# A hybrid delta-rule and pooling block: lowest doubling level on 32x32 diagonal tiles, and first projection tiles run between token turns

## The chip, the core and the metric
One core of a Trainium2 chip runs the kernel. The metric is device time in microseconds (us) of one execution. Engines: TensorE (PE), VectorE (DVE), ScalarE (ACT), GpSimd (POOL), SyncE (SP, which issues most DMAs).

## What is computed
A block on 1024 tokens of width 1024, with 16 meta tokens ahead of them, all float32: a mixer (gated delta rule plus a pooling branch), a gated MLP of width 2816, and a last norm. Of the mixer, per chunk of 64 rows (the kernel takes two such chunks, 128 rows, at a time), the part that the change touches:
```python
lower = jnp.where(strict, jnp.einsum('bhncd,bhnsd->bhncs', kb, k) * decay, 0.0)
tinv = lax.linalg.triangular_solve(lower + eye, eye, left_side=True, lower=True, unit_diagonal=True)
u = jnp.einsum('bhncs,bhnsv->bhncv', tinv, v * beta[..., None])
w = jnp.einsum('bhncs,bhnsd->bhncd', tinv, kb * jnp.exp(g)[..., None])
```
and in front of it `u = rms_norm(h)`, `proj = u @ w_in` (8 tiles of 128 columns each of q, k, v, after a causal convolution of 4 taps and SiLU; beta and decay rates; z; pool input; two gates), and behind it `y = g_a * y_a + g_b * y_b` and `y @ w_out`.

## The kernel before, in words
**Precision and units.** Each float32 factor is split into a high and a low part; a product is three matmuls: high by high, high by low, low by high. `unit` (line 702, matmul line 709) makes one weight tile of 128 features times one block of 342 to 348 tokens: 8 x 3 = 24 matmuls. A tile has three blocks. ScalarE makes the high part of a weight tile (`w_high`, line 1029), GpSimd the low (`w_low`, line 605).

**Front.** Nine groups of tokens (the meta tokens and eight of 128) are normed: ScalarE sums squares and takes the root (lines 1033, 1035), VectorE scales into xs (lines 1372, 1374), TensorE transposes (line 722), ScalarE copies to u_hi (line 1054), VectorE makes u_lo (line 1386). Then TensorE runs tile AB (beta and decay), and 24 q, k, v tiles (`project`, line 738) with a turn of the tile before behind each (`turn`, line 744), then four pool tiles. The preparation of chunk 0 (`FIRST_PLAN`) follows, interleaved with the pool products.

**Loop.** Eight iterations. Each runs the recurrence of chunk i (steps P1, V, O, SU, OT) and the preparation of chunk i+1, in the order of STEPS: P1, TKN, V, TKB, GROW, KK, TQ, TKG, O, SU, QK, TQD, OT, X0, Y0, X1, Y1, X2, Y2. Between the steps TensorE runs pieces (8, 9 or 6 of the 72 matmuls of three k ranges) of nine z and gate projection units, as many behind a step as FILLS (line 133) says. Units 3 to 5 are the first gate: ScalarE takes their sigmoid (line 1234), and behind unit 5 VectorE multiplies zs by gs (line 1618).

**The inverse.** KK gives at_m, the strictly lower product, 128x128 per head for 8 heads. Its eight 16x16 diagonal blocks per head are inverted by forward substitution on GpSimd (`substitute`, line 638; 64 rows, one per head and block). They go there and back through DRAM: SyncE's `invert` (line 466) stores 8 blocks, loads them as rows, stores the solutions and loads 8 blocks into bd, whose other elements are zero. Chunk 0 takes one block alone, since all rows but the last 16 are padding. From 16 to 128 there are three doubling levels, each a product X and a product Y: level 0 joins blocks of 16 into 32 (X0, Y0), level 1 gives 64, level 2 gives 128. X0 = at_m by bd, Y0 = X0 (masked to level 0, nmx) by rr, each a full 128x128 product per head (`product`, MATMUL line 814, 8 MATMULs in two halves of 4, each as two passes: 16 in the trace). rr is bd transposed in 32x32 squares by VectorE (line 1511). X1 and Y1 use 32-column tiles on 32 MATMULs and 48 in the trace (lines 840, 848, 850); X2 and Y2 use 64-column ones (lines 853, 856). Steps are ordered between engines by semaphores: s_bd (block load landed), s_rr (rr transposed), s_ps (product in PSUM), s_ev (its result read and stored), s_tt, s_rd, s_gfree.

```python
elif name == "X0":
    pe.wait_ge(s_bd, 16 + 16 * BLKS * c)
    each([done["KK"]], product(at_m, bd))
elif name == "Y0":
    pe.wait_ge(s_rr, c)
    each([done["X0"]], product(nmx, rr))
```

## Time and profile before
| what | value |
|---|---|
| median of 3 runs (range) | 1842.59 us (1842.28 to 1844.46) |
| the profiled execution | 1844.31 us |
| its span in the profile | 1842.5 us |
| TensorE busy | 1753.2 us, 95% |
| VectorE, ScalarE, GpSimd busy | 951.0, 634.5, 485.8 us |
| mean granted clock of TensorE | 0.987 |
| one loop iteration | 61.3 us, of which TensorE is busy 59.88 |

All durations below come from the one profiled execution; what of its time lies outside the span is 1.8 us. The busy share of an engine is an average; what a stage waits for is read from the chain of waits and the timelines.

### The profile page before, as it was taken

To read this page: it belongs to the slowest core of one execution; us is meant where nothing else is said; L and a number is where in the kernel's file an instruction comes from. 1 tells how busy PE (TensorE), PEld (TensorE's weight loads), DVE (VectorE), ACT (ScalarE), POOL (GpSimd) and SP (SyncE) were. 2 spreads that over 40 slices of the span, in tenths; PEclk is the share of its full clock that TensorE was granted. 3 is DMA by queue.
4 is the path that set the end of the run, shared out by engine and by line. 5 is a ranking of instruction groups with operands and counts; after the bars stand their busy time and mean duration, and the time that the engine had idled before them with its cause. 6 is when DMAs were issued, how large, how long until landed. Compare 5 with 4: busy or idle time off the path is not lost.

```text
span 1842.5 us, 30292 instructions
## 1 busy us (share of the span) xinstructions
PE 1753.2 (95%) x11793; PEld 1680.6 (91%) x11793; DVE 951.0 (52%) x1068; ACT 634.5 (34%) x1026; POOL 485.8 (26%) x468
## 2 busy tenths in 40 slices
PE   5999999986999999999978989999999999999997
PEld 4999999985999999999978989899899999999996
DVE  5344545562556655665553256454564554455457
ACT  6544443344353335333522243112222122122213
POOL 3222222123333434343411113212212122122120
PEclk9999999998999999999989999999999999999999
DMA  6133323224223422342377111111111111111112
GB/s 185 56 90 88 94 84 97 86 81 149 64 74 105 117 63 74 105 117 63 74 239 229 35 35 58 46 34 57 46 34 57 46 34 59 44 46 57 34 46 91
DMA packets 189850, 147.00 MB, mean 80 GB/s; under 512 B 22940, under 2 KB 178115, under 8 KB 188660
## 3 DMA queue, kind: packets, MB, share of 16 engines
q1 hardware_dynamic: 148740, 114.88, 21.4%
q10 hardware_dynamic: 40848, 31.49, 5.5%
q8 instruction: 25, 0.41, 0.1%
q0 software_dynamic: 224, 0.12, 0.0%
q14 instruction: 13, 0.11, 0.0%
HBM read 109.72 MB, written 36.74 MB: 79 GB/s over the span
## 4 chain that ended last, share of the span: by engine, by line
PE 85%; DVE 5%; issue 3%; DMA 2%; ACT 2%; POOL 1%; DVEq 1%; POOLq 1%; SPq 0%; ACTq 0%
PE gb L709 60%; PE db L987 12%; PE db L814 5%; PE db L811 2%; PE db L750 1%; DMA yo<-ot_d 1%; PE db L866 1%; PE db L865 1%; DVE hx L1677 1%; DVE nmx L1539 1%; DVE form L1466 0%; PE db L940 0%; DVE fino L1783 0%; PE db L722 0%; ACT hx L1033 0%
## 5 line engine op out<-in xcount | busy, mean ns | idle before, releaser
L709 PE MATMUL gb<-u_hi,w_hi 128*128 128x342 f32 (+2 forms) x2520 | 824.3, 327 | 18.6 <-ACT ht L1275 7.4
L709 PE MATMUL gb<-u_lo,w_hi 128*128 128x342 f32 (+2 forms) x2520 | 810.5, 322 | 0.0
L709 PE MATMUL gb<-u_hi,w_lo 128*128 128x342 f32 (+2 forms) x2520 | 807.4, 320 | 0.0
L605 POOL TENSOR_TENSOR w_lo<-w_raw,w_hi 128x1024 fp32r<-128x1024 f32 x128 | 338.2, 2648 | 1082.3 <-ACT w_hi L1029 1082.3
L709 PEld LDWEIGHTS gb<-u_hi,w_hi 128*128 128x128 f32 x2520 | 478.3, 190 | 22.1 <-issue 19.3
L709 PEld LDWEIGHTS gb<-u_lo,w_hi 128*128 128x128 f32 x2520 | 478.4, 190 | 0.5
L709 PEld LDWEIGHTS gb<-u_hi,w_lo 128*128 128x128 f32 x2520 | 477.8, 190 | 0.0
L1749 DVE TENSOR_TENSOR h<-h,db 128x512 f32<-128x512 f32 x176 | 117.1, 684 | 59.0 <-PE db L987 58.6
L987 PE MATMUL db<-w_hi,a_hi 128*128 128x512 f32 x352 | 140.7, 400 | 2.9 <-DVE a_lo L1773 2.9
L1029 ACT ACTIVATE w_hi<-w_raw 128x1024 fp32r<-128x1024 f32 x128 | 133.6, 1052 | 18.1 <-ACT tm L1098 13.4
L987 PE MATMUL db<-w_hi,a_lo 128*128 128x512 f32 x352 | 139.7, 397 | 0.0
L987 PE MATMUL db<-w_lo,a_hi 128*128 128x512 f32 x352 | 139.6, 397 | 0.0
L1410 DVE SCALAR_TENSOR_TENSOR cacc<-xb,prm,cacc 128x1040 f32<-128x1040 f32 x72 | 109.0, 1514 | 11.3 <-issue 10.6
L1316 ACT ACTIVATE a_hi<-cv 128x1024 fp32r<-128x1024 f32 x21 | 22.3, 1060 | 249.0 <-PE db L987 202.1
L1301 ACT ACTIVATE xv<-gb 128x342 f32<-128x342 f32 x63 | 28.8, 456 | 188.0 <-PE gb L709 188.0
L1703 DVE TENSOR_SCALAR cg<-xg,prm 128x1024 f32<-128x1024 f32 x22 | 16.6, 754 | 140.3 <-ACT xg L1301 135.7
L1407 DVE TENSOR_SCALAR cacc<-xb,prm 128x1040 f32<-128x1040 f32 x24 | 18.3, 762 | 133.9 <-ACT xb L1117 133.9
L1234 ACT ACTIVATE gs<-gb 128x342 f32<-128x342 f32 x48 | 21.9, 456 | 189.7 <-PE gb L709 189.7
L987 PEld LDWEIGHTS db<-w_hi,a_hi 128*128 128x128 f32 x352 | 66.6, 189 | 21.8 <-DVE h L1749 3.6
L1117 ACT ACTIVATE xb<-gb 128x346 f32<-128x346 f32 (+1 forms) x72 | 33.0, 459 | 144.8 <-PE gb L709 144.1
L987 PEld LDWEIGHTS db<-w_hi,a_lo 128*128 128x128 f32 x352 | 66.6, 189 | 15.9
L987 PEld LDWEIGHTS db<-w_lo,a_hi 128*128 128x128 f32 x352 | 66.5, 189 | 15.0
(226 smaller groups left out, 1962.6 us busy)
## 6 DMA issues: line engine op xcount, KB each, us to landing
w_raw<-in_w_in SPq DMA_DIRECT2D x53, 512.0 KB, 3.9
w_raw<-in_w_up SPq DMA_DIRECT2D x44, 512.0 KB, 3.8
qkv_d<-tm ACTq DMA_DIRECT2D x24, 576.0 KB, 3.1
tk<-qkv_d SPq DMA_DIRECT2D x9, 1536.0 KB, 8.5
w_raw<-in_w_down SPq DMA_DIRECT2D x22, 512.0 KB, 3.3
ot_d<-ots ACTq DMA_DIRECT2D x9, 512.0 KB, 3.2
yb_d<-ybs ACTq DMA_DIRECT2D x8, 513.0 KB, 3.8
yl<-yb_d SPq DMA_DIRECT2D x8, 513.0 KB, 5.2
```

The costliest lines, as they stand in the source:

```text
L605: pool.tensor_tensor(w_lo[:, n % SLOTS, :], w_raw[:, n % SLOTS, :], w_hi[:, n % SLOTS, :].bitcast(F32), ALU.subtract).then_inc(s_wlo, 1)
L709: mm = pe.matmul(gb[:, bank, 0:w], wt, u, start=(k == 0 and m == 0), stop=(k == KT - 1 and m == 2))
L811: return lambda o, m: pe.transpose(o, src[:, m, :], ident)
L814: return lambda o, m: pe.matmul(o, a[:, m, :], b[:, m, :], start=True, stop=True)
L987: mm = pe.matmul(db[:, u % 4, :], a, wt, start=(q == 0 and m == 0), stop=(q == 1 and m == 2))
L1029: act.activation(w_hi[:, n % SLOTS, :], w_raw[:, n % SLOTS, :], ACT.Copy).then_inc(s_whi, 1)
L1117: act.activation(xb[:, j % 3, 3 + o:3 + o + w], gb[:, b, 0:w], ACT.Copy).then_inc(s_gfree, 1)
L1234: act.activation(gs[:, o:o + w], gb[:, b, 0:w], ACT.Sigmoid).then_inc(s_gfree, 1)
L1301: act.activation(dst[:, o:o + w], gb[:, b, 0:w], ACT.Copy).then_inc(s_gfree, 1)
L1316: act.activation(a_hi[:, q, :], cv[:, :], ACT.Copy).then_inc(s_ahi, 1)
L1410: t = dve.scalar_tensor_tensor(cacc[:, :], xb[:, slot, j:j + T], tap(j), cacc[:, :], ALU.mult, ALU.add)
L1749: dve.tensor_tensor(dst, dst, db[:, u % 4, :], ALU.add).then_inc(s_dnfree, 1)
```

## The change
**Lowest level.** bd is replaced by a compact bds of [128, 8 heads, 32]: the 32x32 diagonal squares alone. X0 and Y0 become 32x32 products on diagonal tiles of TensorE (4 squares by 8 heads, 32 MATMULs in the code each, 64 counted as two passes); their results lie in one PSUM bank, so VectorE masks or subtracts once for 8 heads on 32 columns. X1 and Y1 use compact squares too, X2 and Y2 64-row and 64-column tiles. Ahead of each half of a tiled step stands a wait on a constant semaphore (`settled`). ScalarE spreads the squares out into rr and tth with six copies (s_rd). X0 waits for s_rr, the transpose of bds on VectorE, where it waited for the load s_bd.
**Transfers.** `invert` stores 4 diagonal squares, loads twice, stores twice, loads once: 9 DMAs for 18. Chunk 0 does all eight blocks where it did one, with the DRAM copy zeroed first; GpSimd clears rr behind the substitution.
**Fills.** Behind OT stand 2 pieces for 5, behind X1 and Y1 2 for 1, behind X2 1 for 0.
**Front.** The first tiles AB, q0 and q1 run block by block from the time that tokens 0 to 3 are normed, with the turns of tokens 4 to 8 between half units. Constants are loaded in two parts, the identity ahead, the rest later. The weight copies on ScalarE (`w_high`) stand behind tokens 2, 3 and 5; sigmoid and softplus for beta and decay move behind q, k, v tiles 15 to 17.

The diff, cut to its core:
```diff
 FILLS = {"P1": 2, "TKN": 0, "V": 1, "TKB": 0, "GROW": 1, "KK": 2, "TQ": 2, "TKG": 2, "O": 2, "SU": 2, "QK": 1,
-         "TQD": 1, "OT": 5, "X0": 1, "Y0": 2, "X1": 1, "Y1": 1, "X2": 0, "Y2": 1}
+         "TQD": 1, "OT": 2, "X0": 1, "Y0": 2, "X1": 2, "Y1": 2, "X2": 1, "Y2": 1}
...
-            sp.dma_start(cst[:, :], consts).then_inc(s_const, 16)
+            sp.dma_start(cst[:, C_ID:C_ID + P], consts[:, C_ID:C_ID + P]).then_inc(s_const, 16)
...
+                if j in (4, 6):
+                    load_w(W_QKV + j // 2 - 2, cols(w_in, (j // 2 - 2) * P))
+            sp.dma_start(cst[:, P:], consts[:, P:]).then_inc(s_const, 16)
...
-            def invert(c, n=BLKS):
...
+            def by_rows(m):
+                return m.rearrange("(h p) c -> p h c", h=HEADS)
+            def sub_blocks(m, e):
+                return m.rearrange("(g e r) (f c) -> e f g r c", e=2, r=SUB, f=2)[e][e]
+            def sub_rows(m, e):
+                n = BLKS * HEADS // 2
+                return m[e * n:(e + 1) * n, :].rearrange("g (r c) -> g r c", r=SUB)
+            def invert(c):
                 sp.wait_ge(s_ev["KK"], 2 * c + 2)
-                for b in range(n):
-                    sp.dma_start(rows(blk_d, b), block(BLKS - n + b, at_m)).then_inc(s_bst, 16)
-                sp.wait_ge(s_bst, stored + 16 * n)
-                sp.dma_start(blk[0:HEADS * n, :], blk_d[0:HEADS * n, :]).then_inc(s_blk, 16)
+                for p in range(P // SQ):
+                    sp.dma_start(by_rows(blk_d)[square(p)], at_m[square(p), :, square(p)]).then_inc(s_bst, 16)
+                sp.wait_ge(s_bst, 16 * (P // SQ) * (c + 1))
+                for e in range(2):
+                    sp.dma_start(sub_rows(blk, e), sub_blocks(blk_d, e)).then_inc(s_blk, 16)
                 sp.wait_ge(s_sol, c + 1)
-                sp.dma_start(sol_d[0:HEADS * n, :], sol[0:HEADS * n, :]).then_inc(s_sst, 16)
-                sp.wait_ge(s_sst, 16 * c + 16)
-                if n < BLKS:
-                    sp.wait_ge(s_zero, 4)
-                for b in range(n):
-                    sp.dma_start(block(BLKS - n + b, bd), rows(sol_d, b)).then_inc(s_bd, 16)
+                for e in range(2):
+                    sp.dma_start(sub_blocks(sol_d, e), sub_rows(sol, e)).then_inc(s_sst, 16)
+                sp.wait_ge(s_sst, 32 * c + 32)
+                sp.dma_start(bds[:, :, :], by_rows(sol_d)).then_inc(s_bd, 16)
...
+            sp.wait_ge(s_zero, 4)
+            sp.dma_start(by_rows(sol_d), bds[:, :, :]).then_inc(s_sz, 16)
+            sp.wait_ge(s_sz, 16)
+            invert(0)
...
-            substitute(0, 1)
+            substitute(0)
             w_low(W_ZG + 2)
             pool.wait_ge(s_gfree, U_ZG)
             pool.wait_ge(s_yb[0], 16 * 4)
             pool.wait_ge(s_yb[1], 16 * 4)
+            pool.memset(rr[:, :, :], 0.0).then_inc(s_zero, 1)
...
+            later = list(range(FIRST_TOKENS[0] + 1, KT + 1))
             for b, (o, w) in enumerate(BLOCKS):
-                unit(W_AB, b, o, w).then_inc(s_g, 1)
+                for n in range(3):
+                    q = 3 * b + n
+                    w_ready(W_AB + n)
+                    if q >= 3:
+                        pe.wait_ge(s_gfree, q - 2)
+                    for hf in range(2):
+                        if later:
+                            turn_tokens(later.pop(0))
+                        if n == 0 and hf == 0:
+                            pe.wait_ge(s_u, 2 * (FIRST_TOKENS[b] + 1))
+                        mm = unit(W_AB + n, n, o, w, 4 * hf, 4 * hf + 4)
+                    mm.then_inc(s_g, 1)
...
+            project(W_QKV + 2, U_QKV + 6, blocks=(0, 1))
+            turn(0, True)
+            project(W_QKV + 2, U_QKV + 6, blocks=(2,))
+            turn(1)
...
+            def settled():
+                pe.wait_ge(s_const, 32)
...
+                def squares(inputs, op):
+                    for h in range(2):
+                        settled()
+                        if freed:
+                            pe.wait_ge(s_ev[freed[0]], freed[1] + h + 1)
+                        for s, v in inputs:
+                            pe.wait_ge(s, v + h + 1)
+                        for m in range(4 * h, 4 * h + 4):
+                            t = op(db[:, bank, m * SQ:(m + 1) * SQ], m)
+                        t.then_inc(s_ps[name], 1)
...
-                    pe.wait_ge(s_bd, 16 + 16 * BLKS * c)
-                    each([done["KK"]], product(at_m, bd))
-                elif name == "Y0":
+                    settled()
                     pe.wait_ge(s_rr, c)
-                    each([done["X0"]], product(nmx, rr))
+                    def lower(o, m):
+                        for p in range(P // SQ):
+                            t = pe.matmul(o[square(p), :], at_m[square(p), m, square(p)], bds[square(p), m, :],
                                           start=True, stop=True)
                         return t
+                    squares([done["KK"]], lower)
+                elif name == "Y0":
+                    def upper(o, m):
+                        for p in range(P // SQ):
+                            t = pe.matmul(o[square(p), :], xms[square(p), m, :], rrs[square(p), m, :],
+                                          start=True, stop=True)
+                        return t
+                    squares([done["X0"]], upper)
...
+                if j in (2, 3, 5):
+                    w_high(W_AB + (2, 3, 5).index(j))
+                elif j == 6:
+                    act.wait_ge(s_hd, 32)
+                    act.wait_ge(s_zero, 3)
+                    ab_taken(0)
...
+                elif name == "Y0":
+                    act.wait_ge(s_ps["V"], 2 * c)
+                    act.wait_ge(s_tt, c)
+                    for p in range(2):
+                        act.activation(tth[square(p), :, square(p)], tts[square(p), :, :], ACT.Copy)
+                    for p in range(P // SQ):
+                        t = act.activation(rr[square(p), :, square(p)], rrs[square(p), :, :], ACT.Copy)
+                    t.then_inc(s_rd, 1)
...
+                elif name == "X0":
+                    dve.wait_ge(s_bd, 16 * c + 16)
+                    dve.wait_ge(s_rd, c)
+                    dve.transpose(rrs[:, :, :], bds[:, :, :]).then_inc(s_rr, 1)
+                    dve.wait_ge(s_ps[name], 2 * c)
+                    dve.tensor_tensor(xms, dsquares(name), cst[:, C_LV:C_LV + SQ].unsqueeze(1).broadcast_to(
+                        [P, HEADS, SQ]), ALU.mult).then_inc(s_ev[name], 2)
+                elif name == "Y0":
+                    dve.wait_ge(s_ps[name], 2 * c)
+                    dve.tensor_tensor(rrs[:, :, :], rrs[:, :, :], dsquares(name), ALU.subtract).then_inc(s_ev[name], 2)
+                    drain()
+                    dve.transpose(tts, rrs[:, :, :]).then_inc(s_tt, 1)
```

VectorE (DVE) in the loop, from the product of QK (qkm) to the first product after X0; before:
```order
L1596 RECIPROCAL tiny<-tiny 128x8 [waits s_ort]
L1599 TENSOR_TENSOR vb<-vb,tiny 128x1024 [waits s_ev_O]
L1617 ISA
L1618 TENSOR_TENSOR zs<-zs,gs 128x1026 [waits s_gfree]
L1550 ISA
L1511 STREAM_TRANSPOSE rr<-bd 128x1024 [waits s_ps_V,s_bd]
L1553 TENSOR_TENSOR nmx<-db,cst 128x512 [waits s_ps_X0] x2
L1558 TENSOR_TENSOR rr<-rr,db 128x512 [waits s_ps_Y0]
```
and now:
```order
L1683 RECIPROCAL tiny<-tiny 128x8 [waits s_ort]
L1686 TENSOR_TENSOR vb<-vb,tiny 128x1024 [waits s_ev_O]
L1708 ISA
L1709 TENSOR_TENSOR zs<-zs,gs 128x1026 [waits s_gfree]
L1628 STREAM_TRANSPOSE rrs<-bds 128x256 [waits s_rd,s_bd]
L1630 TENSOR_TENSOR nmx<-db,cst 128x8x32 [waits s_ps_X0]
L1634 TENSOR_TENSOR rrs<-rrs,db 128x256 [waits s_ps_Y0]
L1636 STREAM_TRANSPOSE nmx<-rrs 128x8x32
```
The transpose stands where it stood, behind the product of zs (zs by gs, which waits for s_gfree, the sigmoid of unit 5). It is 256 columns wide and not 1024, and X0's result is masked in one instruction.

TensorE (PE) around X0 in the loop; db is the product's PSUM bank, gb the projections'. Before:
```order
L709 MATMUL gb<-u_hi,w_hi 128x342
L709 MATMUL gb<-u_lo,w_hi 128x342
L709 MATMUL gb<-u_hi,w_lo 128x342
L831 ISA
L814 MATMUL db<-bd,at_m 128x128 [waits s_ev_KK,s_ev_TQD,s_bd]
L814 MATMUL db<-bd,at_m 128x128 x3
L814 MATMUL db<-bd,at_m 128x128 [waits s_ev_KK,s_ev_TQD]
L814 MATMUL db<-bd,at_m 128x128 x3
L900 REGISTER_ALU
L709 MATMUL gb<-u_hi,w_hi 128x342 [waits s_gfree]
L709 MATMUL gb<-u_lo,w_hi 128x342
```
and now:
```order
L717 MATMUL gb<-u_hi,w_hi 128x342
L717 MATMUL gb<-u_lo,w_hi 128x342
L717 MATMUL gb<-u_hi,w_lo 128x342
L875 MATMUL db<-bds,at_m 32x32 [waits s_ev_TQD,s_const,s_ev_KK,s_rr]
L875 MATMUL db<-bds,at_m 32x32 x15
L875 MATMUL db<-bds,at_m 32x32 [waits s_ev_KK,s_ev_TQD,s_const]
L875 MATMUL db<-bds,at_m 32x32 x15
L708 REGISTER_ALU
L957 REGISTER_ALU [waits s_wlo]
L717 MATMUL gb<-u_hi,w_hi 128x342 [waits s_gfree]
L717 MATMUL gb<-u_lo,w_hi 128x342
L717 MATMUL gb<-u_hi,w_lo 128x342
```
X0 has 32 instructions where it had 8, and waits for s_rr (VectorE's transpose) where it waited for s_bd; ahead of it stand 15 projection matmuls behind OT where there were 39.

TensorE (PE) in the front, from the last token group's transposes (before) and from token group 4's (now) on. Before:
```order
L722 MATMUL db<-cst,xs 128x128 [waits s_u]
L722 MATMUL db<-cst,xs 128x128 x3
L728 MATMUL mb<-cst,prow 128x105 [waits s_prow]
L728 MATMUL mb<-cst,prow 128x88
L728 MATMUL mb<-cst,prow 128x44
L709 MATMUL gb<-u_hi,w_hi 128x346 [waits s_wlo,s_u]
L709 MATMUL gb<-u_lo,w_hi 128x346
L709 MATMUL gb<-u_hi,w_lo 128x346
```
and now:
```order
L729 MATMUL db<-cst,xs 128x128 [waits s_u,s_xs,s_wlo]
L729 MATMUL db<-cst,xs 128x128 x3
L729 MATMUL db<-cst,xs 128x128 [waits s_u]
L729 MATMUL db<-cst,xs 128x128 x3
L717 MATMUL gb<-u_hi,w_hi 128x346 [waits s_u]
L717 MATMUL gb<-u_lo,w_hi 128x346
L717 MATMUL gb<-u_hi,w_lo 128x346
L717 MATMUL gb<-u_hi,w_hi 128x346
L717 MATMUL gb<-u_lo,w_hi 128x346
L717 MATMUL gb<-u_hi,w_lo 128x346
L717 MATMUL gb<-u_hi,w_hi 128x346
L717 MATMUL gb<-u_lo,w_hi 128x346
```
The first projection matmul stood behind the transposes of all nine token groups and of the parameters; now it stands behind those of token 4, and the later groups' transposes stand between its halves.

## Rows read from the trace of the kernel before
**Rows 1.** The page, the chain that ended last, by line
```profile
PE gb L709 60%; PE db L987 12%; PE db L814 5%; PE db L811 2%; PE db L750 1%; DMA yo<-ot_d 1%; PE db L866 1%; PE db L865 1%; DVE hx L1677 1%; DVE nmx L1539 1%; DVE form L1466 0%; PE db L940 0%; DVE fino L1783 0%; PE db L722 0%; ACT hx L1033 0%
```

**Rows 2.** The chain of waits, loop, 577 to 640 us: start, length, what
```profile
610.20 6.15 PE gb L709 x39
616.35 1.78 PE db L814 x16
...
619.57 1.78 PE db L814 x16
...
623.72 0.63 PE db L840 x32
...
625.97 0.15 PE db L848 x2
...
626.61 1.62 PE gb L709 x9
628.23 0.41 PE db L853 x8
...
630.02 0.45 PE db L856 x8
```

**Rows 3.** Timeline of VectorE, 609 to 634 us: start, length, instruction, idle before
```profile
613.10 2.27 DVE L1618 TENSOR_TENSOR zs<-zs,gs 128x1026 f32<-128x1026 f32 x1 [4.88 <-ACT gs L1234]
615.30 1.23 DVE L1511 STREAM_TRANSPOSE rr<-bd 128x1024 f32<-128x1024 f32 x1
...
632.23 1.23 DVE L1622 TENSOR_TENSOR gs<-gs,yl 128x1026 f32<-128x1026 f32 x1 [1.11 <-ACT gs L1234]
```

**Rows 4.** Timeline of ScalarE, then of GpSimd, same stretch
```profile
612.62 0.46 ACT L1234 ACTIVATE gs<-gb 128x342 f32<-128x342 f32 x1 [1.73 <-PE gb L709]
612.97 1.05 ACT L1029 ACTIVATE w_hi<-w_raw 128x1024 fp32r<-128x1024 f32 x1
...
612.40 1.90 POOL L635 TENSOR_TENSOR vb<-tk,fac 128x1024 f32<-128x1024 f32 x1
```

**Rows 5.** Timeline of SyncE's issues, 580 to 616 us
```profile
585.34 3.66 SPq L478 DMA_DIRECT2D blk_d<-at_m  x8
...
607.32 3.62 SPq L487 DMA_DIRECT2D bd<-sol_d  x8
```

**Rows 6.** Timeline of VectorE, 5 to 30 us
```profile
9.87 0.15 DVE L1372 RECIPROCAL tiny<-tiny 16x1 f32<-16x1 f32 x1 [9.87 <-DMA gmix<-in_norm_mix]
```

**Rows 7.** The chain of waits, 0 to 100 us
```profile
21.41 1.98 PE db L722 x8
...
37.52 37.15 PE gb L709 x216
...
88.10 11.45 PE gb L709 x72
```

**Rows 8.** Windows, TensorE: length, busy (count), clock, DMA share, GB/s
```profile
3.00:9.80 6.80, 0.00 (x0) 1.00 0.92 285
37.52:42.88 5.36, 5.36 (x18) 1.00 0.61 163
42.88:74.67 31.79, 31.79 (x201) 1.00 0.14 40
```

**Rows 9.** Timeline of TensorE behind gaps; last line: the window there
```profile
415.10 0.39 PE L791 MATMUL gb<-p_hi,w_hi 128*128 128x342 f32 x1 [1.34 <-ACT ybs L1171]
...
974.55 0.39 PE L709 MATMUL gb<-u_hi,w_hi 128*128 128x342 f32 x1 [3.69 <-ACT ht L1275]
...
1087.37 0.44 PE L709 MATMUL gb<-u_hi,w_hi 128*128 128x342 f32 x1 [2.26 <-issue]
...
1087.60:1091.00 3.40, 3.40 (x13) 0.50 0.03 7
```

**Rows 10.** Timeline of GpSimd, 405 to 440 us
```profile
408.19 0.95 POOL L663 MEMSET bd<- 128x1024 f32 x1
...
425.87 0.20 POOL L653 TENSOR_TENSOR upd<-blk,sol 8x15 f32<-8x15 f32 x1 [11.03 <-DMA blk<-blk_d]
```

More of the change, by code:

```diff
@@ L160 @@
                                 if OBLOCKS[b][0] < _cols)
+FIRST_TOKENS = [-(-(o + w - META) // P) for o, w in BLOCKS]
 NORMED = [-(-(o + w - HALO) // P) + 1 for o, w in OBLOCKS]
@@ L711, in unit, with turn_tokens @@
                 return mm
-            pe.wait_ge(s_const, 16)
-            for j in range(KT + 1):
+            def turn_tokens(j):
                 pe.wait_ge(s_xs, j + 1)
@@ L851, in step @@
-                    each([done["X1"], done["Y0"]], right_squares)
+                        return pe.matmul(o[square(1), :], rrs[square(1), m, :], xms[square(1), m, :],
+                                         start=True, stop=True)
+                    squares([done["X1"], done["Y0"]], right_squares)
                 elif name == TOP_X:
+                    settled()
+                    pe.wait_ge(s_rd, c + 1)
                     each([done["Y1"]], lambda o, m: pe.matmul(
-                        o[side(m), 0:HALF], at_m[:, m, HALF:], tt_m[:, m, 0:HALF], start=True, stop=True))
+                        o[side(m), 0:HALF], at_m[0:HALF, m, HALF:], tth[:, m, :], start=True, stop=True), True)
@@ new lines, in _ @@
+            for b in range(3):
+                if b:
+                    ab_taken(b)
+                if b == 2:
+                    w_high(W_QKV + 2)
+                for n in range(2):
+                    qkv_taken(n, b)
+                    if b == 2:
+                        w_high(W_QKV + 3 + n)
+                if b == 0:
+                    act.wait_ge(s_prmT, 1)
+                    for r, (p0, m) in enumerate(((0, R_CF), (R_CF, 88), (R_CF + 88, 44))):
+                        act.activation(prm[:, p0:p0 + m], mb[:, r * P:r * P + m], ACT.Copy).then_inc(s_prm, 1)
@@ L1121, in qkv_tile @@
                     by_tokens(n - 1, squared)
-            act.wait_ge(s_zero, 3)
-            for j in range(3):
-                qkv_tile(j)
+            for b, (o, w) in enumerate(BLOCKS):
+                act.wait_ge(s_g, U_QKV + 6 + b + 1)
+                act.activation(xb[:, 2, 3 + o:3 + o + w], gb[:, b, 0:w], ACT.Copy).then_inc(s_gfree, 1)
+                if b == 0:
+                    silu(0)
+                elif b == 1:
+                    by_tokens(0, True)
+                    silu(1)
+            by_tokens(1, True)
             with act.Fori(0, 4) as i:
@@ L1128, in _ @@
                     qkv_tile(j, i)
-            for j in range(15, 18):
+            for j, part in ((15, beta_sigmoid), (16, softplus_parts), (17, softplus_log)):
                 qkv_tile(j, squared=j <= 2 * HEADS)
+                part()
             with act.Fori(0, 2) as i:
@@ L1604, in _ @@
             dve.wait_ge(s_bd, 16)
-            turned_squares(rr, bd).then_inc(s_ev[LAST_Y], 2)
+            dve.wait_ge(s_zero, 5)
+            for p in range(P // SQ):
+                t = dve.transpose(rr[square(p), :, square(p)], bds[square(p), :, :])
+            t.then_inc(s_ev[LAST_Y], 2)
+            dve.drain().then_inc(s_rd, 1)
             def gated(u, i):
```

216 lines of the change are left out of this document (101 added, 115 removed).

## The prediction
> **What bounds the kernel now.** I read the page's chain first. Projection matmuls (line 709) and products of the up and down projections (line 987) hold 72% of the span [rows 1]: TensorE sets the time, so a part of the change counts only where it makes TensorE work less, wait less, or run at another clock. Then I read the chain through one loop iteration [rows 2]: the lowest level is two lumps of 16 MATMULs, X0 at 616.35 and Y0 at 619.57, 1.78 us each, behind a fill of 39 projection matmuls of 6.15 us. What X0 needs is on the other engines' timelines [rows 3 to 5]. The same for the front [rows 6 to 8] and for chunk 0 [rows 10]; rows 9 show what a gap on TensorE costs beyond itself. The sum is made against the profiled execution, 1844.31 us (span 1842.5). That is 1.7 above the median of the three runs, 1842.59, so the forecast is the sum less 1.7. About 0.2% of it, 3.7 us, is what a measurement can tell from no change.
>
> **The transfers.** A chunk had 18 block transfers and gets 9. The eight stores took 3.66 us to issue and the eight loads 3.62, 0.457 each [rows 5]. The last load is issued at 610.94; X0 starts at 616.35 behind its fill and its data had landed (its chain step names projection matmuls, no DMA). So their end is covered by the fill, and the nine that go are worth **nothing** in the loop. If the fill that covers them goes too, the four stores and one load that remain still end earlier (about 5 us of issue saved), so DMA is not late next.
>
> **The loop, 8 times.** *X0's wait.* Before, TensorE waits for the block load alone, VectorE transposes bd meanwhile, and only Y0 waits for it. Now X0 waits for s_rr, so for that transpose, and VectorE issues it behind the product of zs. That product waits for the sigmoid of projection unit 5 (612.62, 0.46 us [rows 4]), whose last piece is the second of the fills behind OT. These 15 matmuls end at 610.20 + 15 x 0.158 = 612.57; the 24 others, until now between OT and X0 (3.8 us), move behind X1, Y1 and X2. The product runs 613.10 to 615.37 [rows 3]; the transpose is 1.23 us for 1024 columns, for 256 I take 0.35. X0 can start at 615.7 where TensorE is ready at 612.57: **a stall of 3.1 us** that nothing covers, since X0's fills stand behind it in program order. Bounds: the product takes 2.27 us beside GpSimd's vb product (612.40 to 614.30), and a product of the same size takes 1.23 with GpSimd idle (632.23) [rows 3, 4]. So 2.1 to 3.3 us.
> *X0 and Y0.* 64 tile MATMULs each in place of 16. Y1 has 48 MATMULs in the 0.64 us from 625.97 to 626.61, 13.3 ns each, X1 32 in 0.63, 19.7 ns each [rows 2]; 64 give 0.85 or 1.26 us. I take 0.85, Y1's price, as X0 and Y0 have full rounds of four tiles: 2 x (1.78 - 0.85) = **-1.86 us**; bounds -1.0 and, if the rounds cost no more than Y1 as a whole (0.64), -2.3.
> *X2 and Y2.* From X2's start at 628.23 to Y2's end at 630.47 pass 2.24 us, 0.86 of it work [rows 2]: TensorE waits for VectorE's copies. A piece of fill moved there covers about 0.95 of it: **-0.95** (0 to -1.3).
> *Seams.* X0 and Y0 become tiled steps: +0.1 for two more changes of shape (0 to 0.4); the constant-semaphore wait ahead of each half has long been met. ScalarE gets six copies before V of the next chunk, with its 0.46 us sigmoids [rows 4] far apart: nothing.
> Together +3.1 - 1.86 - 0.95 + 0.1 = +0.4 per iteration, **+3.2** for eight (0 to +10).
> The Trainium skill ("TensorEngine Tiling (Array Packing)", Key Properties) says that a change of tiling mode drains TensorE. Two more tiled steps would pay that; no row here prices it alone, and the sum does without it.
>
> **The clock.** X0's stall is a gap of a size that TensorE doesn't have in the loop now. Each gap in the trace of 2.26 us or more was followed by a stretch at half clock: 2.26 us before 1087.37, 3.69 before 974.55; the window behind the first is at a granted clock of 0.50, 1.2 GHz of 2.4, with 13 matmuls in 3.40 us, where 0.158 each gives 2.05. The gap of 1.34 us before 415.10 was not followed by one: its matmuls follow at full rate [rows 9]. A stall of 3.1 us with half a microsecond of small products around it is on the far side. I take a fall in 6 of 8 iterations at 1.4 us: **+8.4** (0 to +14).
>
> **The front.** Before, nine tokens are turned first and 216 matmuls (three tiles) run from 37.52 to 74.67 [rows 7], the first 18 in 5.36 us, 201 more in 31.79, 0.158 each [rows 8]. Now the first starts once tokens 0 to 3 are done and token 4 is turned. Token 4's transposes end at 21.41 + 1.98 = 23.4 [rows 7]. VectorE's first instruction waits for gmix until 9.87 [rows 6], behind the whole constants (128 x 832 numbers, 0.43 MB), most of which now go later: at the 285 GB/s of that stretch [rows 8], -1.4. A w_hi copy of 1.05 us [rows 4] enters ScalarE's queue ahead of token 3's norm: +1.05. So dense work starts at 23.0, and the tiles end at 23.0 + 216 x 0.158 (34.2) + 2.5 for the low-clock start + 5.0 for four token turns between (one at 1.98, three at half that) + 0.4 for the parameter transposes + 0.5 of waits = 65.6. From there to the tile that starts at 88.10 [rows 7] it was 13.4 us; it is that plus about 0.7, as ScalarE and VectorE get first tiles closer together: 79.75. **-8.4** (-3 if tokens are slowed by copies between them; -10.5 at best). Softplus and sigmoid move to between tiles 15 and 17: three to six ScalarE passes of a 1040-column row, about 1.05 us each by the nearest copy [rows 4], covered by tiles of 11.45 us: +0.4 (0 to 1).
>
> **Chunk 0's substitution.** Before, GpSimd clears bd (0.95) and can start the substitution only when one block has come, after 11.03 us of waiting [rows 10]. Now three more stores are issued (3 x 0.457 = 1.4), a second load (0.46), and rr's clearing stands ahead of kd and vb (1024 columns like bd, 0.95): **+2.7** (1.5 to 4). The chain of the end of the preparation runs through GpSimd's substitution, kd and vb and the tk load behind them, so no TensorE work covers it.
>
> **The end of the loop.** The last za store goes later with unit 5's product where the fills moved, and the y phase's loads wait for it: +0.3 (0 to 3).
>
> **Sum.** -8.4 + 0.4 + 2.7 + 3.2 + 8.4 + 0.3 = **+6.6**: 1850.9 against 1844.31, 1849.2 against the median. Without the clock term it is -1.8.
>
> **Rivals.**
> *B, the stall comes but the clock holds.* For: small products and tile steps lie near it, and only gaps of 2.26 us and more are known to bring a fall. Against: 3.1 is above them all. -1.8: 1840.8, no change.
> *C, the stall is short: faster.* Its place is VectorE's product of zs. If GpSimd's vb product is out of its way, it takes 1.23, not 2.27; the stall is 2.1, under every gap with a fall, and TensorE keeps 2.4 GHz. With Y1's whole price, 0.64, for X0 and Y0: 2.1 - 2.28 - 0.95 + 0.1 = -1.0 per iteration, -8.3, and the sum -13.3: 1829.3. It decides from the point where the stall is below some 2.2 us. For it: only two engines' order has to shift by a microsecond; against it: GpSimd's queue is not changed there.
> *D, the front stays at 1.2 GHz for longer.* Turns and waits stand between the first units; if some 43 more matmuls run at 0.298 (5.36 / 18 [rows 8]) and not 0.158, +6: 1855.
> *E, MATMULs can't come as close as I take them.* At 25 ns apart X0 and Y0 would take 1.6 us each, 1.5 more per iteration, +12: 1861. X1's 19.7 ns and Y1's 13.3 [rows 2] speak against it. The Trainium skill ("TensorE: Matmul & The Clock Gate", "Wait — 56ns, not 53.3ns?") has the rule that start-to-start never falls below about 25 ns; by these rows the trace disagrees.
> *The change doesn't do what it says* in that its fewer transfers were hidden: that is in the forecast already.
>
> **How the numbers follow.** Forecast 0.43, B 0.27, C 0.18, D 0.07, E 0.05. The forecast's own bounds (clock in 3 to 8 iterations, loop term 0 to 10) reach from 1842 to 1858. With B's, which start at about 1836, and a part of C down to 1832, the range 1832 to 1858 leaves out half of C, most of D and E, and the forecast's far ends: 2 in 10. Faster by over 3.7 us: C and the lower end of B, 0.25. Within: the rest of B and the forecast's low end, 0.28. Slower: 0.47.
>
> **What would show it.** Right: X0 starting right behind the 256-column transpose, TensorE idle about 3 us before it in each iteration, a window at 0.50 behind it in most; X0 and Y0 at 0.85 us; dense work from 23 us and the third tile's end near 65.6; the first step after chunk 0's preparation 2.7 us later relative to KK. Wrong: a loop period of 61.3 us or less (then the stall or the fall is absent), GpSimd's vb product not beside the product of zs, X0 above 1.3 us, or a front that gains under 3 us.

## The result, and the profile after

The changed kernel takes 1854.27 us (median of 5 runs, 1851.73 to 1855.20), the kernel before 1843.11 (5 runs, 1842.28 to 1845.83). The ratio is 1.0055, with a 95% interval of 1.0041 to 1.0070: the change makes the kernel slower by 0.55%, some 10 us. The profiled execution of the changed kernel took 1854.41 us, with a span of 1852.6. Against the span of before, 1842.5, 10.1 us are to be explained.

From the page of the changed kernel, its busy times, the row of the granted clock in 40 slices, and the chain that ended last:

```profile
span 1852.6 us, 31814 instructions
...
PE 1742.2 (94%) x12561; PEld 1669.7 (90%) x12561; DVE 915.4 (49%) x1007; ACT 663.3 (36%) x1081; POOL 483.5 (26%) x470
...
PEclk9999999998999999999979999999999999999999
...
PE 79%; DVE 6%; issue 6%; DVEq 3%; DMA 2%; ACT 2%; POOL 1%; POOLq 1%; SPq 0%; ACTq 0%
PE gb L717 59%; PE db L1044 8%; PE db L853 3%; DVEq L1459 3%; PE db L850 2%; PE db L770 1%; DVE h L1840 1%; DMA yo<-ot_d 1%; PE db L923 1%; PE db L922 1%; DVE cacc L1496 1%; DVE hx L1768 1%; POOL w_lo L614 1%; DVE form L1556 0%; PE db L997 0%
```

TensorE is busy 11 us *less* (1742.2 us against 1753.2), and the span is 10 us longer. In the chain its share fell from 85% to 79%, and "issue", time in which an engine waits for nothing that the profile shows, rose from 3% to 6%; projection matmuls hold 59% of it and held 60 [rows 1]. The loss is not more work.

The chain through the loop iteration that [rows 2] show of before (start, length, what):

```profile
606.79 2.37 PE gb L717 x15
609.16 3.26 issue
612.42 1.07 PE db L875 x64
613.49 2.60 PE gb L717 x9
616.09 0.68 PE db L883 x50
616.77 2.57 PE gb L717 x15
619.34 0.62 PE db L893 x32
...
626.21 0.61 PE db L909 x16
...
628.45 0.61 PE db L912 x16
```

X0 (line 875) starts at 612.42; the 15 matmuls behind OT end at 609.16. TensorE stands idle for 3.26 us. (The chain can list fewer MATMULs than the code has: "x50" below is a whole step of 64 as well.) VectorE's timeline says for what:

```profile
609.69 2.28 DVE L1709 TENSOR_TENSOR zs<-zs,gs 128x1026 f32<-128x1026 f32 x1 [4.87 <-ACT gs L1327]
611.88 0.43 DVE L1628 STREAM_TRANSPOSE rrs<-bds 128x256 f32<-128x256 f32 x1
```

The zs product waits for ScalarE's sigmoid and takes 2.28 us, as in [rows 3]; the transpose behind it ends at 612.31, and X0 follows 0.1 us later. Then the clock; windows of TensorE (length, busy (count), granted clock, DMA share, GB/s), the first and third behind X0 in this iteration, the second in the iteration before:

```profile
612.40:615.40 3.00, 2.98 (x71) 0.50 0.91 352
547.80:554.40 6.60, 6.57 (x143) 0.52 0.56 220
616.00:619.00 3.00, 3.00 (x79) 1.00 0.14 57
```

TensorE ran at 0.50 of its clock, 1.2 GHz, behind X0: "613.49 2.60 x9" is 9 matmuls in 2.60 us, where [rows 8] give 1.4. This happened in all eight iterations: five times for 3.4 us, three times for 6.8 (the window from 547.80 is one of the long ones). Below, such a stretch at 0.50 is called a fall. Before, no loop window is under 1.00.

The iteration's length is read from the start of the zs product on VectorE. Where the 10.1 us come from, from the same marks in the two traces:

| stretch | before | after | difference |
|---|---|---|---|
| start to q, k, v tile 3 | 88.10 | 77.76 | -10.3 |
| to the first zs product | 490.51 | 481.69 | -8.8 in all, +1.5 here |
| seven iterations of the loop | 7 x 61.30 | 7 x 63.69 | +16.8 |
| last zs product to the first a_lo of the down projection | 200.1 | 206.3 | +6.2 |
| rest of the up and down projections, last norm | 722.8 | 718.8 | -4.0 |

The last row is a stage whose code nothing touched.

The front, from the chain (first two lines) and TensorE's timeline:

```profile
22.26 3.25 PE gb L717 x12
...
77.76 11.45 PE gb L717 x72
...
76.56 1.21 PE L770 MATMUL db<-cst,sl 128*128 128x128 f32 x9 [1.33 <-ACT sl L1164]
```

Dense work starts at 22.26 (37.52 in [rows 7]), and tile 3 at 77.76 (88.10). VectorE's first instruction, which waited for gmix until 9.87 [rows 6], starts at 7.23. The first three tiles, 216 matmuls, end at 62.8 (74.68 in [rows 7]). The turn of tile 1 waits 1.33 us for ScalarE's SiLU, behind VectorE's second convolution.

GpSimd's timeline where chunk 0 is prepared:

```profile
415.85 0.21 POOL L659 TENSOR_TENSOR upd<-blk,sol 64x15 f32<-64x15 f32 x1 [11.09 <-DMA blk<-blk_d]
...
430.35 0.94 POOL L678 MEMSET rr<- 128x1024 f32 x1
```

The substitution starts 10.0 us earlier than in [rows 10], of the 10.3 that the front had won; the three added stores and the second load cost 0.3 us together. The clearing of rr costs its 0.94.

### The profile page after: what moved, and what is told of

Its sections match the earlier page's. It is cut to its first block, busy times and chain, and to the rows that moved or that the text cites. A ratio compares the mean times of both kernels' runs of the same rounds, so it can differ in the third digit from the quotient of the medians.

```text
span 1852.6 us, 31814 instructions
## 1 busy us (share of the span) xinstructions
PE 1742.2 (94%) x12561; PEld 1669.7 (90%) x12561; DVE 915.4 (49%) x1007; ACT 663.3 (36%) x1081; POOL 483.5 (26%) x470
## 4 chain that ended last, share of the span: by engine, by line
PE 79%; DVE 6%; issue 6%; DVEq 3%; DMA 2%; ACT 2%; POOL 1%; POOLq 1%; SPq 0%; ACTq 0%
PE gb L717 59%; PE db L1044 8%; PE db L853 3%; DVEq L1459 3%; PE db L850 2%; PE db L770 1%; DVE h L1840 1%; DMA yo<-ot_d 1%; PE db L923 1%; PE db L922 1%; DVE cacc L1496 1%; DVE hx L1768 1%; POOL w_lo L614 1%; DVE form L1556 0%; PE db L997 0%
## 5 line engine op out<-in xcount | busy, mean ns | idle before, releaser
L717 PEld LDWEIGHTS gb<-u_hi,w_hi 128*128 128x128 f32 x2520 | 482.2, 191 | 23.9 <-issue 20.8
L659 POOL TENSOR_TENSOR upd<-blk,sol 64x15 f32<-64x15 f32 (+4 forms) x135 | 39.9, 296 | 144.8 <-DMA blk<-blk_d 126.9
L1796 DVE SCALAR_TENSOR_TENSOR cg<-xg,prm,cg 128x1024 f32<-128x1024 f32 x22 | 70.2, 3190 | 3.5 <-issue 3.4
```

The lines of the kernel that those rows point to most:

```text
L659: pool.tensor_tensor(out, low[:, j, j + 1:].unsqueeze(2).broadcast_to([n, rest, j + 1]), inv[:, j, 0:j + 1].unsqueeze(1).broadcast_to([n, ...
L717: mm = pe.matmul(gb[:, bank, 0:w], wt, u, start=(k == 0 and m == 0), stop=(k == KT - 1 and m == 2))
L1796: dve.scalar_tensor_tensor(dst[:, c0:c1], src[:, c0 + 1:c1 + 1], tap(1), dst[:, c0:c1], ALU.mult, ALU.add)
```

## The experiments

Two theories stand against each other. **S, the stall:** the loss is X0's wait behind the zs product and the half clock that the wait brings. **T, the tiles:** 64 tiny MATMULs in a row leave TensorE nearly idle, and the clock falls for them, whatever stands ahead. Kernels that ran together share their runs of the kernel before, whose medians in the three groups were 1844.55, 1843.07 and 1843.81 us.

### e1: the old fills

```diff
-         "TQD": 1, "OT": 2, "X0": 1, "Y0": 2, "X1": 2, "Y1": 2, "X2": 1, "Y2": 1}
+         "TQD": 1, "OT": 5, "X0": 1, "Y0": 2, "X1": 1, "Y1": 1, "X2": 0, "Y2": 1}
```

> The changed kernel with the old table of fills (5 pieces behind OT, 1 behind X1 and Y1, 0 behind X2). Theory S (the stall): the loss of the loop is X0's wait for VectorE's transpose behind the zs product (3.26 us) and the half clock that follows it. 39 matmuls (6.15 us) cover that wait again, so no low clock behind X0, X0 and Y0 still cost less than before: period about 59.5 us (63.7 with the change, 61.3 before), time about 1820. Theory T (the tiles): TensorE falls to half clock because 64 tiny tile MATMULs leave it nearly idle, whatever stands ahead. Then the clock still falls in most iterations, period about 61.5 to 62, time about 1836 to 1840.

Measured: 1824.86 us (1823.21 to 1827.77), ratio to before 0.9892 (0.9871 to 0.9912). The iterations take 59.5 us as expected, except for the first, 62.56; the time is 5 us over the 1820 of theory S. The first iteration has no wait before X0 either, but a gap of 1.45 us in a fill before 490.90, whose cause is open, and 1.5 us after its end the clock falls. The window there:

```profile
492.43:495.80 3.37, 3.37 (x43) 0.50 0.02 5
```

It is the only window of the loop under 1.00. The chain around X0 in the second iteration:

```profile
541.89 5.37 PE gb L717 x34
547.26 0.68 PE db L875 x50
547.95 1.61 PE gb L717 x9
549.56 0.68 PE db L883 x50
550.24 2.54 PE gb L717 x15
```

No wait ahead of X0, and X0 and Y0 take 0.68 us each, not 1.78 [rows 2]. One line of the fill table turns +0.6% into -1.1%. Theory S is right in the period; T is out, since the same tiles run at full clock in seven of eight iterations, and in the first one too until a gap. The rows also show a cost that I had put at 0.1 us: the 9 matmuls behind X0 take 1.61 us and the 15 behind Y0 2.54, where 0.158 us each [rows 8] make 1.42 and 2.37; behind X1 and Y1, which were tiled before too, 9 took 1.62 [rows 2]. Each switch from tiles to dense work costs some 0.18 us. The Trainium skill ("TensorEngine Tiling (Array Packing)", Key Properties) says that changing the tiling mode drains TensorE. The 0.18 us fit that; whether they are a drain, the trace does not show.

### e2: the transpose ahead of the zs product

```diff
                     dve_step(name, i if name in REC else i + 1)
+                    if name == "OT":
+                        dve.wait_ge(s_bd, 16 * (i + 1) + 16)
+                        dve.wait_ge(s_rd, i + 1)
+                        dve.transpose(rrs[:, :, :], bds[:, :, :]).then_inc(s_rr, 1)
                     for u in units_after(name):
```

with the same three lines taken out of X0's step.

> The changed kernel, with VectorE's transpose of bds (the one that X0 waits for) ahead of the zs product instead of behind it. bds has landed 4 us before. Theory S: no wait before X0; a wait of about 1.2 us moves before Y0, whose mask now stands behind the zs product; this is short, so the clock holds: period about 59.6 us, time about 1820. Theory T: the clock still falls behind X0; period 61.5 or more, time 1836 or more.

Measured: 1824.75 us (1822.82 to 1825.81), ratio 0.9886 (0.9867 to 0.9906); period 59.75, clock 1.00 throughout the loop. VectorE's timeline:

```profile
596.79 0.45 DVE L1721 STREAM_TRANSPOSE rrs<-bds 128x256 f32<-128x256 f32 x1 [0.56 <-DMA bds<-sol_d]
601.11 2.27 DVE L1706 TENSOR_TENSOR zs<-zs,gs 128x1026 f32<-128x1026 f32 x1 [3.87 <-ACT gs L1327]
603.30 0.41 DVE L1627 TENSOR_TENSOR nmx<-db,cst 128x256 f32<-128x256 f32 x1
```

The transpose runs in VectorE's idle time and ends before TensorE comes to X0. The product now holds up only X0's mask (603.30) and with it Y0, by 0.98 us, where 1.2 was expected. Another way to remove the same wait gives the same time as e1: the wait is the cause, not where the fills stand.

### e3 and e7: the stall filled with useless work

```diff
                     for p in pieces_after(name):
                         piece(p, i)
+                    if name == "OT":
+                        for r in range(18):
+                            pe.matmul(mb[:, 0:342], u_hi[:, r % 8, 0:P], u_hi[:, r % 8, 0:342], start=True, stop=True)
```

e7 has `range(9)`. The added matmuls write a PSUM bank that nothing reads there. e3 leaves 0.45 us of idle time before X0, e7 about half of the stall.

> The changed kernel with 18 matmuls of 128x342 into an unused PSUM bank before X0, about 2.85 us of work without use that fits into the stall of 3.26 us. Theory S: the stall's own time stays, the low clock behind it goes: 2.0 us less per iteration, period about 61.7, time about 1838. Theory T (or: the stall itself is all of the loss and the clock is innocent): the clock falls still, or its fall costs nothing; time about 1853.

> The changed kernel with 9 matmuls of no use ahead of X0 where the run before had 18: TensorE stands idle about 1.85 us before X0, not 3.26 and not 0.45, and X0's start stays where it is. If the length of the idle gap decides the fall, a gap between the 1.3 us (none in the kernel before) and the 2.3 us (always): likely none, period 62.1, time 1842. If any wait ahead of the small tiles is enough: half clock in most iterations, period 63 or more, time 1850.

Measured: e3 1842.73 us (1838.82 to 1847.19), ratio 0.9987 (0.9975 to 1.0000). X0 starts no earlier, but the clock stays at 1.00 in all eight iterations; the chain:

```profile
607.41 2.80 PE mb L978 x18
610.21 0.45 issue
610.66 0.74 PE db L875 x48
611.40 1.62 PE gb L717 x9
```

2.80 us of work without use per iteration save 11.5 us in all. The period is 62.06 (after the first), against 63.3 with a short fall and 64.5 with a long one: a fall of 3.4 us costs 1.3 us, one of 6.8 us 2.5 us. e7 took 1844.08 us (1840.57 to 1845.76), ratio 1.0006 (0.9996 to 1.0015). From TensorE's timeline:

```profile
605.21 1.56 PE L978 MATMUL mb<-u_hi 128*128 128x342 f32 x9
608.62 0.74 PE L875 MATMUL db<-bds,at_m 32*32 32x32 f32 x64 [1.84 <-issue]
```

With an idle gap of 1.84 us the clock fell in 3 of 8 iterations, for 3.4 us each; the periods are 62.0 without and 63.4 with. I had expected likely none, so the gap that is safe is shorter than I took from the two gaps of [rows 9] (1.34 us, no fall; 2.26 us, a fall).

### e4: the front alone

The front's hunks of the change (tiles between token turns, split constants, moved sigmoid and softplus) put on the kernel before, the rest as it was:

```diff
+            later = list(range(FIRST_TOKENS[0] + 1, KT + 1))
             for b, (o, w) in enumerate(BLOCKS):
-                unit(W_AB, b, o, w).then_inc(s_g, 1)
+                for n in range(3):
...
+            project(W_QKV + 2, U_QKV + 6, blocks=(0, 1))
+            turn(0, True)
+            project(W_QKV + 2, U_QKV + 6, blocks=(2,))
+            turn(1)
```

> The kernel before with the front of the change alone (tiles between token turns, split constants, moved softplus), its loop and its transfers as before. The changed kernel's trace shows tile 3 of q, k, v starting 10.3 us earlier than before. Both theories: loop period 61.3 with no low clock; time 9 to 10 us less than before, about 1833 to 1834. If the gain of the front is given back before the loop, less than 5 us remain.

Measured: 1837.46 us (1835.47 to 1839.10), ratio 0.9951 (0.9932 to 0.9970): 7.1 us less, not 9 to 10. Its chain has tile 3 at

```profile
78.22 11.45 PE gb L711 x72
```

9.9 us earlier than before, and the first zs product is 9.0 us earlier, the last 9.2. From there to the first a_lo it takes 203.3 us where before it was 200.1: 3 us of the gain are given back between the loop and the down projection. That stretch takes between 195.7 and 206.3 us over the kernels of this study.

Half of those 3 us are the clock. At the start of the up projections all 13 kernels have the same two gaps on TensorE, 2.26 us and, 12 to 14 us later, 1.62. TensorE's timeline and the window at the second gap in the changed kernel, then the window there before:

```profile
1114.11 0.63 PE L717 MATMUL gb<-u_hi,w_hi 128*128 128x342 f32 x1 [1.62 <-issue]
1114.11:1117.40 3.29, 3.29 (x12) 0.50 0.00 0
...
1101.49:1105.00 3.51, 3.51 (x22) 1.00 0.00 0
```

From the end of the first gap to the first a_lo it takes 33.9 us in the seven kernels whose clock falls at both gaps (e4 and the changed kernel are among them) and 32.3 in the six where it falls at one (the kernel before is one): 1.5 us. The other 1.6 us of e4's loss lie ahead of these gaps, where DMAs of yo, yz and yg are waited for; what sets them was not tried.

### e5: e2 with one fill moved

```diff
-         "TQD": 1, "OT": 2, "X0": 1, "Y0": 2, "X1": 2, "Y1": 2, "X2": 1, "Y2": 1}
+         "TQD": 1, "OT": 2, "X0": 2, "Y0": 1, "X1": 2, "Y1": 2, "X2": 1, "Y2": 1}
```

> The changed kernel with VectorE's transpose ahead of the zs product and one fill piece moved from behind Y0 to behind X0 (2 and 1 where they were 1 and 2), so that the wait of 1.2 us before Y0 is covered. Theory S: no wait in the doubling levels, period 58.6 to 58.8 us (59.75 without the moved piece), time about 1816. If the wait only moves on to X1 (VectorE's subtraction and second transpose, about 1.1 us), period 59.2 or more and time 1820 or more.

Measured: **1814.64 us** (1813.10 to 1816.26), ratio 0.9852 (0.9834 to 0.9871), the fastest version, 28 us under the kernel before. Period 58.84. Its chain:

```profile
594.74 2.37 PE gb L717 x15
597.11 0.68 PE db L875 x50
597.80 3.04 PE gb L717 x18
600.83 0.68 PE db L883 x50
601.51 1.15 PE gb L717 x6
...
602.71 0.69 PE db L893 x31
```

From OT's fill to X1 the largest wait left is the 0.05 us between 602.66 and 602.71.

### e6: GpSimd's product out of the way

```diff
+                if not isinstance(c, int):
+                    pool.wait_ge(s_zg, c)
                 pool.tensor_tensor(vb[:, :, :], tk[:, 2 * HEADS:, :], per_head(factor(FV, c)),
```

This is rival C's condition, on the changed kernel.

> The changed kernel with GpSimd's vb product held back until VectorE's zs product is done. If the zs product is long (2.27 us) because GpSimd works beside it, it takes about 1.23 us now and X0's stall falls from 3.26 to 2.2 us. Rival C of the prediction says that the clock then holds: period about 61.0, time about 1832. If gaps of 2.2 us still bring the fall: period 62.6, time 1845. If the length of the product has nothing to do with GpSimd: stall and period as with the change, 63.7, time 1853.

Measured: 1834.06 us (1833.86 to 1835.24), ratio 0.9957 (0.9943 to 0.9972). VectorE's zs product, and TensorE's X0:

```profile
606.12 1.23 DVE L1711 TENSOR_TENSOR zs<-zs,gs 128x1026 f32<-128x1026 f32 x1 [4.87 <-ACT gs L1329]
...
607.81 1.08 PE L877 MATMUL db<-bds,at_m 32*32 32x32 f32 x64 [2.21 <-issue]
```

The product takes 1.23 us where it took 2.28 beside GpSimd's, and the gap before X0 is 2.21 us where it was 3.26. The clock fell in 4 of the 8 iterations (periods of 62.3, against 61.0 in the others): a result between the two that I had named, and 20 us faster than the changed kernel for one wait on GpSimd, which is busy a quarter of the time.

### e8: where the tiles lie in SBUF

On e1:

```diff
-C_INV = C_LV + 32
+C_INV = C_LV + 3 * P
```

> The changed kernel with the old fills (median 1824.9), and with 96 unused columns of constants, as many as the kernel before had: every tile behind them in SBUF lies at its old address again. In the unchanged up and down projections, a pair of tiles takes 39.1 + 28.25 us with the change and 39.4 + 28.25 before, 3 us over the stage. If addresses in SBUF cause it, the step returns to 39.4 and the time is about 1828; if the program's other length or order does, it stays at 39.1 and 1825.

Measured: 1828.08 us (1825.30 to 1829.52), ratio 0.9923 (0.9903 to 0.9944), 3.2 us above e1. Two starts of a_lo in the down projection in e8, then in e1:

```profile
1323.84 1.23 DVE L1833 TENSOR_TENSOR a_lo<-cv,a_hi 128x1024 fp32r<-128x1024 f32 x1 [1.13 <-ACT a_hi L1409]
...
1363.28 1.23 DVE L1833 TENSOR_TENSOR a_lo<-cv,a_hi 128x1024 fp32r<-128x1024 f32 x1 [0.41 <-ACT a_hi L1409]
```

```profile
1323.55 1.23 DVE L1833 TENSOR_TENSOR a_lo<-cv,a_hi 128x1024 fp32r<-128x1024 f32 x1 [1.13 <-ACT a_hi L1409]
...
1362.67 1.23 DVE L1833 TENSOR_TENSOR a_lo<-cv,a_hi 128x1024 fp32r<-128x1024 f32 x1 [0.41 <-ACT a_hi L1409]
```

The step is 39.44 us with the wide constants and 39.12 with the narrow ones; it is 39.4 in all ten such steps of the kernel before, of e4 and of e11, which have the wide constants, and 39.1 in the changed kernel and all others, which have the narrow ones. Ten steps are the 3.2 us. But for a wider load of the constants, the instructions of e8 are those of e1; what differs is that every tile behind the constants lies 1408 bytes further on (352 columns, not the 96 of the expectation). Which tile's address counts was not tried.

### e9 and e10: are the transfers worth something?

Nine more stores per chunk ahead of the real ones, 18 transfers as before, on e1 (e9) and on e5 (e10):

```diff
+                for r in range(0 if isinstance(c, int) and c == 0 else 9):
+                    n = HEADS * SQ
+                    sp.dma_start(dup_d[r * n:(r + 1) * n, :].rearrange("(h p) c -> p h c", h=HEADS),
+                                 at_m[square(r % 4), :, square(r % 4)]).then_inc(s_bst, 16)
                 for p in range(P // SQ):
```

> The changed kernel with the old fills (median 1824.9), and nine more block stores per chunk in the loop, to a scratch tensor and ahead of the four real ones: 18 transfers per chunk as before, about 4.1 us more of SyncE's time before the blocks go out. VectorE's transpose waits there for the zs product until 6 us after the load landed. So nothing: period 59.5, time 1825. If the transfers were on the path in this order of fills, each 0.457 us of issue would show: up to 4.1 us per iteration.

> The same nine stores in the fastest version so far (transpose ahead of the zs product, one fill piece moved; median 1814.6). There the transpose ends at 593.75 and TensorE comes to X0 at 597.1: 3.35 us of slack against 4.1 us. X0 should wait about 0.8 us: period about 59.6 to 59.8, time about 1821 to 1823. If the fewer transfers are worth nothing in this version too: 58.8 and 1815.

Measured: e9 1821.44 us (1816.18 to 1824.48), period 59.5 after the first, as e1; that it is 3 us below e1 comes from the stretch behind the loop (195.7 us in its trace, 201.6 in e1's; 1.5 of it is one fall fewer at the start of the up projections, the rest is open). e10 took 1853.35 us (1851.11 to 1855.28), 38.7 above e5. VectorE's transpose and TensorE's X0 in e10:

```profile
613.01 0.45 DVE L1726 STREAM_TRANSPOSE rrs<-bds 128x256 f32<-128x256 f32 x1 [6.97 <-DMA bds<-sol_d]
...
613.55 0.74 PE L880 MATMUL db<-bds,at_m 32*32 32x32 f32 x64 [3.16 <-issue]
```

VectorE now waits for the block load, 6.97 us, and TensorE 3.16 us, four times what I had expected: the nine issues take 4.28 us, and from the first store to the end of the transpose it is 30.4 us where e5 needs 23.9. Of these 6.5 us the slack of 3.35 hides half. The gap brings the clock down in all eight iterations (period 64.0). So nine transfers more cost nothing with the old order, and with the new one more than the 28 us that it had gained. All nine stand here ahead of the block stores; the kernel before had eight stores there for four, and eight loads behind the substitution for one, and the price of exactly those in the new order was not measured.

### e11: the kernel before with the change's stall

```diff
-         "TQD": 1, "OT": 5, "X0": 1, "Y0": 2, "X1": 1, "Y1": 1, "X2": 0, "Y2": 1}
+         "TQD": 1, "OT": 2, "X0": 1, "Y0": 2, "X1": 2, "Y1": 2, "X2": 1, "Y2": 1}
...
-                    pe.wait_ge(s_bd, 16 + 16 * BLKS * c)
+                    pe.wait_ge(s_rr, c)
                     each([done["KK"]], product(at_m, bd))
```

> The kernel before, dense 128x128 products and 18 transfers, with two things of the change: its fills (2 pieces behind OT) and X0 waiting for s_rr, VectorE's transpose behind the zs product (1024 columns, 1.23 us). Theory S: a gap of about 4.0 us before X0 in each iteration, and half clock behind it in all or nearly all, though no tile is small: period 66 to 67 us, time about 1880 to 1886. Theory T (the small tiles bring the fall): the gap alone, period about 64.4, time about 1868, no granted clock below 1.00 there.

Measured: 1888.05 us (1886.78 to 1889.52), ratio 1.0241 (1.0224 to 1.0258); period 66.8. TensorE's X0 with its idle time, and the window that starts with it:

```profile
624.71 1.65 PE L814 MATMUL db<-bd,at_m 128*128 128x128 f32 x6 [4.01 <-DVE rr L1510]
...
624.71:630.00 5.29, 5.29 (x23) 0.50 0.92 313
```

A gap of 4.01 us, and half clock behind it in all eight iterations, with dense 128x128 products throughout. Fills and wait alone, without the new tiles, make the kernel before 44 us slower. The fall doesn't need the small tiles in X0 and Y0; e1, e2 and e5 show that without the stall they don't bring it.

The gaps at X0 (Y0 in e2) and the falls there, eight iterations each:

| kernel | idle before X0, us | iterations with a fall | fall of 3.4 / 6.8 us |
|---|---|---|---|
| e1, e5 | none | 0 (e1: one, at the fill's gap) | |
| e3 | 0.45 | 0 | |
| e2 (before Y0) | 0.98 | 0 | |
| e7 | 1.84 | 3 | 3 / 0 |
| e6 | 2.21 | 4 | 4 / 0 |
| e10 | 3.16 | 8 | 4 / 4 |
| changed kernel | 3.26 | 8 | 5 / 3 |
| e11 | 4.01 | 8 | 3 / 5 |

Within one kernel the same gap brings a fall in some iterations and not in others. Gaps elsewhere in the traces show that its length alone does not decide. Of the two at the start of the up projections, the clock falls at the one of 2.26 us in 10 of the 13 kernels (not in e5, e6 and e10), and at the one of 1.62 us in 10 too (not in the kernel before, e9 and e11). A gap in the first iteration's fill is followed by a fall at 1.45 us in e1 and at 2.21 in e9, and by none at 1.93 in e8. Even longer gaps can pass: between the loop and the up projections the clock stays at 1.00 behind 3.15 us before 985.78 in the changed kernel, behind 3.27 in e1 and 3.40 in e6. What else decides is open.

## Why the prediction was right, point by point

The forecast was 1849.2 us, slower, with 1832 to 1858 as the range; 1854.27 was measured. The mechanism of the loss held: X0's stall behind the zs product, and the half clock that it brings. The sizes held less well. Of the span's +10.1 us the sum had +6.6; it was too small by 5.6 for the clock, 2.8 for the loop and 2.6 for the stretch behind it, and too large by 1.9 for the front, 1.6 for tile 3 to the loop and 4.0 for the up and down projections. That these nearly cancel is luck.

**X0's stall.** Forecast 3.1 us, measured 3.26: the transpose of 256 columns takes 0.43 us, not 0.35. Everything else of the wait (unit 5's sigmoid, the product of 2.27) came as it was read from [rows 2 to 4]. e1, e2 and e11 show it as the cause of the loop's loss.

**X0 and Y0.** Forecast 0.85 us each, measured 0.68 at full clock (e1): 64 MATMULs 10.6 ns apart. The bound of 0.64, what Y1 costs as a whole, was the nearer one. The rule of the Trainium skill ("TensorE: Matmul & The Clock Gate", "Wait — 56ns, not 53.3ns?") of about 25 ns from start to start, rival E, is contradicted by these rows as by those of before.

**X2 and Y2.** X2's start to Y2's end is 2.85 us with a fill of 1.62 inside, so 1.2 of its own where it was 2.24: -1.0, forecast -0.95. But the fill between them brings one more switch from tiles to dense work, some 0.18, so about -0.8 is left. e5 (58.84, the changed kernel's fills behind X1, Y1 and X2) against e1 (59.5, the old ones) gives -0.65, with a small wait before X1 in it.

**Seams, and the loop without the clock.** Forecast +0.1 per iteration for seams, measured some 0.18 for each of two tiled steps. With them X0 and Y0 are worth 59.5 - 61.3 = -1.8 (e1), as much as the forecast gave them. 3.26 - 1.8 - 0.8 is some +0.6 per iteration; e3, which keeps the stall and has no fall in the loop, gives 62.06 - 61.30 = +0.76. The forecast was +0.4: over eight, +6 and not +3.2.

**The clock** is the term that was mis-sized most. Forecast: 6 falls of 1.4 us, +8.4. It was 8 falls, 3 of them twice as long: 5 x 1.3 + 3 x 2.5 = 14 us. That a fall can last 6.8 us was in no row of before that I had read, though the trace holds it: the granted clock is 0.50 for 6.8 us from 404.92 and for 10.2 us from 951.05. 14 was the upper bound given. Rival B, that the clock holds, is out. What spoke for it, that only gaps of 2.26 us and more bring a fall, did not hold either: gaps of 1.45, 1.62 and 1.84 us did in some cases.

**Rival C** named the right lever. Its condition, GpSimd's product elsewhere, did not hold in the changed kernel; e6 made it hold and measured 1834.06, where C gave 1829.3. Its sentence that a gap of 2.2 us keeps the clock was wrong in half of the iterations.

**The front.** Forecast -8.4, measured -10.3. Dense work started at 22.26 and not 23.0: gmix came 2.6 us earlier and not 1.4, but the chain then runs through the low part of a weight tile on GpSimd (2.36 us), which the forecast left out. The third tile ended at 62.8 and not 65.6: four turns of about 1.0 us where 5.0 us were given, and 12 slow matmuls in 3.25 us, 1.35 over the full rate, where 2.5 were given. The sum calls these slow first matmuls a low clock; the window of [rows 8] gives 1.00 there, and no run shows the clock as their cause. The wait of the second turn was 1.33 us, forecast 0.7. Rival D did not occur. What I did not forecast is that e4 keeps only 7.1 us of the front's gain.

**Chunk 0.** From tile 3 to the first zs product +1.5, forecast +3.1 (0.4 for the moved sigmoid and softplus, 2.7 for the substitution). The stores and loads cost 0.3 us, not 1.9: from the first store to the first load's issue it was 3.39 us where before it was 2.53 (+0.9, where my sum had 1.4), and from there to the substitution 3.48 where it was 3.98, for which no run gives the reason. rr's clearing cost 0.94, as forecast.

**The y phase** (last zs product to the first a_lo) was forecast at +0.3. The stretch grew by 6.2 us, of which the eighth iteration's stall and fall are 0.76 + 2.5 = 3.3. Of the other 2.9, 1.5 are the second fall at the start of the up projections (e4); 1.4 are open.

**The constants.** I gave the narrower constants a price in the front only. By e8 they are worth 3.2 us in the up and down projections, by address. This gain and the front's set off the clock's and the y phase's loss in the sum.

**The transfers** were forecast at nothing, and e9 bears that out for the old order. e10 limits it: the sentence "DMA is not late next" holds for the nine transfers of the change; with nine more ahead of them, and the transpose early, it is late.

## What to carry to other kernels

A step that is made cheaper can still lose if its input is asked for at another point of a neighbour's program order. Ask of each moved wait what is queued ahead of its producer, and keep independent work ahead of the waiting instruction until the producer is done: a change to the fill table was worth 29 us here, and three moved lines as much. On TensorE a gap costs itself and perhaps the clock behind it. Here gaps of up to 1.0 us in the loop never brought a fall, gaps of 1.45 to 2.26 us did in some cases, and gaps of 3.1 us and more did at X0 each time, though not always elsewhere. A gap of 3 us that can't be removed was worth filling with work that nobody needs (e3, 11.5 us).
